# Rewriting the second block of a two-block transformer kernel: three-pass projections, standing gate weights, head-by-head norms

## The reference

```python
h = rmsnorm(x, norm_pre)
proj = h @ w_in          # qa ka va za | qb kb vb ob zb | ig fg | ga gb
oa = diff_attention(qa, ka, va, lam)          # 4 heads; softmax(1) - lam * softmax(2), ALiBi, causal
ya = rmsnorm_heads(oa, norm_a) * (1 - lam_init) * silu(za)
qk = silu(causal_conv4(concat(qb, kb)))
hb = mlstm(qk_q, qk_k, vb, ig + b_i, fg + b_f)   # 4 heads of 128, decay weights, normalised by max(|den|, exp(-m))
yb = rmsnorm_heads(sigmoid(ob) * hb, norm_b) * silu(zb)
merged = sigmoid(ga) * (ya @ w_a) + sigmoid(gb) * (yb @ w_b)
x = x + rmsnorm(merged @ w_out, norm_post)
```

## Time and profile before

| | |
|---|---|
| median of 3 runs | 1297.14 us (1295.32 to 1297.49) |
| the profiled execution | 1300.73 us, its span 1299.5 us |
| PE, PEld busy | 1246.2 us, 1080.4 us |
| DVE, ACT, POOL busy | 946.0 us, 708.5 us, 57.4 us |
| second block, from its first matmul to the span's end | 258.9 us |

### The profile page before, as it was taken

How to read it: one execution, slowest core, us unless ns; L and a number is a source line. 1 busy time by engine, 2 the same in 40 slices (tenths; PEclk the granted TensorE clock), 3 DMA queues, 4 the chain that set the end, 5 groups by cost and what they waited for, 6 DMA issues and landing times.

```text
span 1299.5 us, 18078 instructions
## 1 busy us (share of the span) xinstructions
PE 1246.2 (96%) x7024; PEld 1080.4 (83%) x7024; DVE 946.0 (73%) x1415; ACT 708.5 (55%) x1082; POOL 57.4 (4%) x80
## 2 busy tenths in 40 slices
PE   7999999986999999999999999999999989999977
PEld 6888888875888888888888888988888878878866
DVE  6787666988687776687776667587775677668976
ACT  5665445663565654565554457556554443655463
POOL 4000000010001000000000112000000000000000
PEclk9999999988999999999999999999999998999999
DMA  8766565410366665666655564156655654555430
GB/s 273 230 201 193 165 189 175 162 61 1 114 195 186 187 185 166 199 191 185 192 178 170 174 194 142 50 177 187 189 186 179 188 154 145 163 142 147 134 126 33
DMA packets 201364, 211.42 MB, mean 163 GB/s; under 512 B 8977, under 2 KB 188305, under 8 KB 201279
## 3 DMA queue, kind: packets, MB, share of 16 engines
q1 hardware_dynamic: 198672, 206.66, 52.2%
q10 hardware_dynamic: 2606, 3.60, 0.8%
HBM read 209.19 MB, written 1.05 MB: 162 GB/s over the span
## 4 chain that ended last, share of the span: by engine, by line
PE 79%; DVE 14%; ACT 3%; issue 2%; DMA 1%; POOL 1%; ACTq 0%; SPq 0%; DVEq 0%
PE psum L468 77%; DVE wlo L1812 4%; DVE cv L2028 2%; ACT whi L1221 1%; POOL small L2664 1%; DMA rows<-in_a_ln_b 0%; PE psum L601 0%; ACT pb L1708 0%; PE psum L882 0%; DMA xn<-in_x 0%; DVE small L2377 0%; DVE htmp L1869 0%; ACT qn L1541 0%; DVE pb L2387 0%; PE psum L629 0%
## 5 line engine op out<-in xcount | busy, mean ns | idle before, releaser
L468 PE MATMUL psum<-x,whi 128*128 128x512 f32 x1952 | 696.9, 401 | 16.3 <-DVE htmp L1869 5.0
L1812 DVE TENSOR_TENSOR wlo<-raw,whi 128x1024 fp32r<-128x1024 f32 (+2 forms) x403 | 473.4, 1188 | 161.4 <-ACT whi L1221 157.8
L468 PE MATMUL psum<-x,wlo 128*128 128x256 f32 x1952 | 548.9, 281 | 0.9 <-DVE wlo L1812 0.9
L1221 ACT CAST whi<-raw 128x1024 fp32r<-128x1024 f32 (+2 forms) x403 | 406.5, 1023 | 147.2 <-PE psum L468 137.2
L468 PEld LDWEIGHTS psum<-x,whi 128*128 128x128 f32 x1952 | 370.5, 190 | 107.6 <-DVE htmp L1869 5.7
L468 PEld LDWEIGHTS psum<-x,wlo 128*128 128x128 f32 x1952 | 372.0, 191 | 1.5 <-DVE wlo L1812 1.4
L468 PE MATMUL psum<-g,whi 128*128 128x512 f32 x704 | 247.0, 394 | 0.0
L468 PE MATMUL psum<-g,wlo 128*128 128x256 f32 x704 | 198.2, 282 | 0.0
L468 PEld LDWEIGHTS psum<-g,whi 128*128 128x128 f32 x704 | 132.3, 188 | 30.6
L468 PE MATMUL psum<-whi,x 128*128 128x512 f32 (+2 forms) x544 | 147.5, 370 | 2.0 <-issue 2.0
L468 PEld LDWEIGHTS psum<-g,wlo 128*128 128x128 f32 x704 | 132.4, 188 | 0.0
(11 more groups left out here) (322 smaller groups left out, 950.1 us busy)
## 6 DMA issues: line engine op xcount, KB each, us to landing
raw<-in_ffn_w_gate SPq DMA_DIRECT2D x88, 512.0 KB, 4.5
raw<-in_ffn_w_up SPq DMA_DIRECT2D x88, 512.0 KB, 4.3
raw<-in_ffn_w_down SPq DMA_DIRECT2D x80, 512.0 KB, 4.2
raw<-in_w_in SPq DMA_DIRECT2D x52, 512.0 KB, 4.0
raw<-in_w_o SPq DMA_DIRECT2D x16, 512.0 KB, 3.9
raw<-in_a_w_in SPq DMA_DIRECT2D x14, 512.0 KB, 4.9
raw<-in_w_kv SPq DMA_DIRECT2D x16, 384.0 KB, 3.3
raw<-in_ffn_w_down SPq DMA_DIRECT2D x16, 256.0 KB, 2.7
```

What stands on the lines that cost most here:

```text
L468: return pe.matmul(o, l, r, start=start, stop=stop, skip_group_check=True)
L1221: act.copy(B.whi[:, i % SPLIT, 0:n], B.raw[:, i % RAW, 0:n]).then_inc(*s.hi.now(i))
L1812: dve.tensor_tensor(B.wlo[:, i % SPLIT, 0:n], B.raw[:, i % RAW, 0:n], B.whi[:, i % SPLIT, 0:n].bitcast(F32), ALU.subtract).then_inc(*s.lo. ...
```

## The change

- **Three passes into one place.** The new `direct` sums `hi*xhi`, `hi*xlo` and `lo*xhi` as three 256-column matmuls into the same half bank; `pair` does this for a slot. All column projections of the second block use it (`QK2`, `AQK2`, `GAB2`, `WA2`, `WB2`). There are no halves to add: DVE reads the bank once and scales it. Column pairs get banks of their own (2, 3, 0, 1 for `QK2`; 6, 7, 2, 3 for `AQK2`; 0, 1, 2, 6 and 7, 4, 5, 6 for `WA2`, `WB2`).
- **Gate columns.** The slot `GATE2` is held 128 columns apart (`held`), and its weights stand in PE: 24 matmuls of 256 columns, then two small transposes (`gate_turn`). The decay sums move ahead of `VA2`.
- **Conv.** The first tap goes to ACT (`tap0`, 8 passes); DVE makes three passes per column.
- **Evictions and functions.** One half of `vb` and one of `va` is read by ACT. ACT's order around `VA2` is new: silu of the conv output, one tiny Exp, then the copy of `va`. `rows_steps` does token tile 0 of a slot, then tile 1, and PE signals the first tile's end (`zo0`). All three `z_fn` now stand between the two kinds of jobs.
- **Fewer DVE operations per job.** `tensor_reduce` with negate gives the bias of the exponential directly; the difference is one pass over p with one ratio; the mLSTM's denominator comes out of the product's accumulator.
- **Norms head by head.** ACT squares each head's output with an accumulator (`y_squares`); the gain is multiplied into z once (`z_gain`), and `y_rows` makes one 128x128 pass per head. `GAB_STEPS` sets how many steps of `rest` go with each mLSTM job; the residual's and the first tile's `yb` turns move in among jobs 8 and 9.

```diff
+GAB_STEPS = (2, 2, 2, 1, 1, 2, 2, 1, 1, 1)
...
+    def direct(o, h, l, xi, kc, start, stop, ready=None):
+        mm(o, h, xh[xi][:, kc, :], start, False)
+        mm(o, h, xl[xi][:, kc, :], False, False)
+        if ready is not None:
+            pe.wait_ge(*s.lo.at(ready))
+        return mm(o, l, xh[xi][:, kc, :], False, stop)
...
-    def gate_rows(x):
+    def gate_cols():
...
-        for tt in range(2):
-            o = bank[5 + tt][:, 0:8]
-            for k in range(8):
-                l0, l1 = (x[q][:, k, tt * 128:(tt + 1) * 128] for q in range(2))
-                mm(o, l0, h[:, k, :], k == 0, False)
-                mm(o, l1, h[:, k, :], False, False)
-                t = mm(o, l0, l[:, k, :], False, k == 7)
+        for k in range(8):
+            t = direct(bank[5][:, 0:S], h[:, k, :], l[:, k, :], 0, k, k == 0, k == 7, i if k == 0 else None)
...
     def rest():            # PE
-                pe.wait_ge(*s.sum.at(("gab", c - 2)))
+                pe.wait_ge(*s.gab.at(c - 2))
-                t = block(6 + c % 2, h[:, k, :], l[:, k, :], x[:, k], k == 0, k == 7, i if k == 0 else None)
+                t = direct(bank[6 + c % 2][:, 0:S], h[:, k, :], l[:, k, :], 0, k, k == 0, k == 7, i if k == 0 else None)
...
     def second():          # ACT
+        for i in range(1, 4):
+            use(VA2 + i)
         for h in range(2):
             silu_cols(h)
+        act.activation(small[0:1, 319:320], B.ones[0:1, 0:1], ACT.Exp)
+        act.wait_ge(*s.used.at(VA2 + 3))
+        act.activation(MC.va[:, 0, :], bank[6], ACT.Copy, scale=small[:, 14:15]).then_inc(*s.v_act.now("va"))
...
+        y_squares("a", 7)
+        next(rg)
         z_fn(1, ACT.Sigmoid)
         z_fn(0, ACT.Silu)
-        for _ in range(2):
-            next(rg, None)
+        next(rg)
+        z_fn(2, ACT.Silu)
+        act.activation(small[0:1, 319:320], B.ones[0:1, 0:1], ACT.Exp)
+        next(rg)
...
     def rest():            # DVE
-            dve.tensor_tensor(g, b[:, 0:S], g, ALU.add).then_inc(*s.sum.now(("gab", c)))
-            dve.wait_ge(*s.sum.at(("gab", c)))
-            dve.tensor_tensor(g, g, row_of(6), ALU.mult).then_inc(*s.gab.now(c))
+            dve.tensor_tensor((MC.ga if c < 8 else MC.gb)[:, c % 8, :], bank[6 + c % 2][:, 0:S], row_of(6),
+                              ALU.mult).then_inc(*s.gab.now(c))
...
     def second():          # DVE, mLSTM jobs
+            for _ in range(GAB_STEPS[i]):
+                next(rg)
+            if i == 1:
+                z_gain(0, 0)
+            if i in (2, 3):
+                y_rows("ya", i - 2)
+            if i in (3, 4):
+                turned("ya", i - 3, 4, 1, 0, [3])
+            if i == 4:
+                z_gain(2, 1)
+            if i == 8:
+                y_rows("yb", 0)
```

More of the change, by code:

```diff
@@ L544, in first_use, with rows_steps @@
             pe.wait_ge(*sig.at((gen, c)))
-    def rows_steps(x, gen, K, slot, n, banks, tail=0):
+    def rows_steps(x, gen, K, slot, n, banks, tail=0, first=None):
         kk = SLOT // n
@@ L567, in rows_steps @@
                                    kc == K - 1 and wi == 1)
+                if first is not None and tt == 0 and k0 + kk == K:
+                    t.then_inc(*s.zo0.now(first))
             t.then_inc(*s.used.now(i))
@@ L1102, in second @@
[L1102 to L1105, removed]
+            if c >= 2:
+                pe.wait_ge(*s.qk.at(c - 2))
+            for e in range(2):
+                pair(0, 0, AQK2 + 2 * c + e, (6, 7, 2, 3)[c], range(4 * e, 4 * e + 4), e == 0, e == 1)
+                if c == 0 and e == 0:
+                    gate_turn()
@@ L1629, in mix_b, with tap0 @@
             prep(5, p, [("f3", 6, xh[0])])
+    def tap0(c):
+        act.wait_ge(*s.qk.at(c))
+        for b in (2 * c, 2 * c + 1):
+            t = act.activation(MC.qkc[:, b, :], MC.qk[:, b, 0:S], ACT.Copy, scale=MC.ctap[:, b, 0:1])
+        t.then_inc(*s.tap0.now(c))
     def silu_cols(h):
@@ L1641, in rest @@
                 if k == 3:
-                    z_rows(i)
+                    act.wait_ge(*s.zo0.at(i))
+                    act.activation(MC.zob[:, i, 0, :], bank[6], ACT.Copy, scale=small[:, 14:15]).then_inc(*s.zo_act.now(i))
                 yield
@@ L2454, in ya_steps, with z_gain @@
-    def ya_steps():
-        yield from head128("ya", flat(MC.oa[:]), flat(MC.zob[:, 0]), MC.nab[:, 0, :], 1.0 - LAM_INIT, 200,
-                           flat(MC.aq[:])[:, 0:1024])
-        for tt in range(2):
-            yield
-            turned("ya", tt, 4, 1, 0, [3])
+        dve.reciprocal(small[:, col + 5:col + 6], small[:, col + 4:col + 5]).then_inc(*s.dve_step.tick())
+    def z_gain(i, norm):
+        dve.wait_ge(*s.z_fn.at(i))
+        dve.wait_ge(*(s.ld_nb if norm else s.ld_na).at("all"))
+        z = MC.zob[:, i]
+        dve.tensor_tensor(z, z, wide(MC.nab[:, norm, :], 1, 2), ALU.mult).then_inc(*s.c_dve.now(("zz", i)))
@@ new lines, in y_rows @@
+    def y_rows(g, tt):
+        b = g == "yb"
+        dve.wait_ge(*s.rstd.at((g, tt) if b else g))
+        dve.wait_ge(*s.c_dve.at(("zz", 2 if b else 0)))
+        src = MC.ob if b else MC.oa
+        for h in range(4):
+            q = slice(h * 128, (h + 1) * 128)
+            c = (224 if b else 208) + 4 * tt + h
+            t = dve.scalar_tensor_tensor(out=src[:, tt, q], in0=src[:, tt, q], scalar=small[:, c:c + 1],
+                                         in1=MC.zob[:, 2 if b else 0, tt, q], op0=ALU.mult, op1=ALU.mult)
+        t.then_inc(*s.y.now((g, tt)))
@@ L2476, in second @@
+        for i in range(6):
+            use(QK2 + i)
+        dve.wait_ge(*s.fills.at("qk"))
+        dve.wait_ge(*s.row.at(6))
+        keys(0)
+        keys(1)
+        use(QK2 + 6)
+        keys(2)
+        use(QK2 + 7)
+        use(GATE2)
+        some(cg, 2)
+        keys(3)
+        some(cg, 2)
+        dve.wait_ge(*s.used.at(GATE2))
+        dve.tensor_tensor(MC.oa[0:8, 0, 0:S], bank[5][0:8, 0:S], row_of(6)[0:8], ALU.mult).then_inc(*s.c_dve.now("g8"))
         l12 = MC.lamr[:, 0:3:2, :]
```

605 lines of the change are left out of this document (287 added, 318 removed).

## The result

| | before | after |
|---|---|---|
| median | 1296.23 us (4 runs, 1293.22 to 1297.49) | 1277.36 us (4 runs, 1275.23 to 1281.34) |
| the profiled execution | | 1279.19 us, its span 1277.8 |
| second block, first matmul to the span's end | 258.9 us | 237.09 us |

The ratio is 0.986, with a 95% interval of 0.983 to 0.990: the changed kernel is faster, by 19 us or 1.5%. I had said 1277. The two profiled executions put all of it into the second block: its first matmul starts at 1040.71 us, against 1040.58, and the block is 21.8 us shorter.

What follows compares the result with a forecast made beforehand. PE was taken as the bound, other engines costing time only where PE waits. Terms -9.9 + 1.7 + 0.4 - 1.3 - 9.9 - 1.5 = -20.5 us took the median from 1297.14 to 1276.6, said as 1277; range 1269 to 1288.

Steps and rivals of the forecast that it cites:

- A: Second block's conv, gate, attention and value projections: 84.29 us to become 74.4, a change of -9.9.
- B: Handover to the jobs: 2.38 us to become 4.1 (+1.7), as PE waits for ACT's table loads, silus and copy.
- C: Difference attention with the row projections, 46.57 us: +0.4 net, with 1.45 for a slow restart and 1.0 off for DVE.
- D: mLSTM with merge-gate columns: 63.48 us to 62.2 (-1.3), including new PE waits of 2.1 at the start and 1.1 in job 5.
- E: Products with w_a and w_b: 33.36 us to become 23.5 (-9.9), with yb ready earlier and the banks free.
- F: Output product, 23.37 us: 96 matmuls give 21.8, and late wlo of the last four slots goes, -1.5.
- G: The tail behind the output product, said to stay at 5.47 us.
- Price of one block: Three 256-column matmuls in place of one 512 and one 256: 0.36 us against 0.347, for 320 blocks.
- gate term of 7.1: In A, the new form of the gate rows saves 4.3 us itself and 2.8 in the column pairs behind them.
- slow start: At the start of C, PE restarts slow after its wait on ACT: +1.45 us, bounds 0 and 1.7.
- ACT's bursts are hidden: Rival, chance 0.12: both PE waits on ACT (3.3 and 2.1) and the slow restart fall away, 6.5 less, 1270.5 us.
- a table load holds ACT twice: Rival, chance 0.04: each table load holds ACT twice as long as its row, 5.1 us more, 1282.

Runs made afterwards that it cites:

- half_columns: Changed kernel with each 256-column matmul of the w_a and w_b products split into two of 128, each with its own weight load: 1294.50 us, E 43.32.
- gate_rows: Changed kernel with only the gate columns put back to 48 matmuls of 8 columns, x standing: 1283.58 us, A 78.99 us, 5.13 longer.
- silu_early: Changed kernel with ACT's two silus and the one-element Exp moved right behind the copy of vb: median 1272.81 us, second block 232.67 us.
- fill_wait: Changed kernel with 26 unused 256-column matmuls run while PE waits for ACT's copy of va: median 1277.06 us, second block 235.75 us.
- zfn_late: Changed kernel with ACT's sigmoid and two silus of z moved behind the last cast and the copy of zob: median 1280.89 us, second block 240.61 us.
- gab_2_passes: Changed kernel with DVE reading each merge-gate slot in two passes instead of one: 1278.66 us, D 4.6 us longer.
- run of four passes: Changed kernel with DVE reading each merge-gate slot in four passes instead of one: 1293.03 us, D 16.5 us longer.

## Why the prediction was right

The mechanism held, and the sum came within 1.3 us: the block lost 21.8 us where I had 20.5. That the median lies within 0.4 us of 1277 is in part luck. I had put it 3.6 below the profiled execution, as before the change; it was 1.8 below. These two misses, 1.3 us one way and 1.8 the other, nearly cancel. Stage by stage, against the earlier trace rows:

| | said | came | |
|---|---|---|---|
| A | 84.29 to 74.4 | 73.86 | 0.5 better |
| B | 2.38 to 4.1 | 4.03 | the burst, row for row |
| C | 46.57 to 47.0 | 46.62 | the 1.0 taken off for DVE was not tried |
| D | 63.48 to 62.2 | 61.58 | the wait in job 5 did not come |
| E | 33.36 to 23.5 | 23.55 | |
| F | 23.37 to 21.8 | 21.95 | |
| G | 5.47 | 5.50 | |

- **Price of one block.** 0.360, as taken from the earlier trace rows; and no run gave 0.33, which follows from the gap that the Trainium skill (TensorE: Matmul & The Clock Gate, "Back-to-back issue gap") states for an isolated warm matmul of 256 columns. The 107 ns for a load that the same page of the Trainium skill states ("LDWEIGHTS (loading the stationary operand)") lie near the 0.111 us that a pass took in half_columns. Against the block's 0.347 the form costs 320 x 0.013 = 4 us; the change pays it for banks that need no second half.
- **A.** Nothing waits and the clock stays at 2.4 GHz throughout. The gate term of 7.1 is only in part the narrow form's own (5.1, run gate_rows); what the other 2 came from stays open. As a difference between the two kernels it stood.
- **B and C.** The wait of 3.3 and the slow start are real and separate (runs silu_early and fill_wait). The slow start costs 1.3 to 1.7 us in eight traces and 2.8 in that of zfn_late (C up to its third row group at 35.14 to 35.39 and 36.61, against 33.74 and 33.81 in silu_early and fill_wait). That the slow start would come was inferred from the wait's length; the waits listed further down show that length alone does not decide it. The rival by which ACT's bursts are hidden falls (its 6.5 should have been 3.3 + 2.1 + 1.45 = 6.85), and so does the one by which a table load holds ACT twice: each function starts 0.02 us or less after its load's 1.28. The drain that the Trainium skill (ScalarE: Activation LUTs, "What ACT_TABLE_LOAD costs") adds is in none of these rows.
- **D.** The wait of 2.02 before the first merge-gate slot was foreseen at 2.1. The 1.1 in job 5 was a term too many; the contents are 61.58 - 2.02 = 59.6 and not 59.0. The 128 blocks of before are 128 x 0.347 = 44.4 and not 44.7, so the old waits by that sum were 6.7; yet PE stood idle for only 63.48 - 60.17 = 3.3 of it, and where the rest lay is not shown. That DVE would no longer pace D was right, but the margin was thinner than I had it: without the 16 passes saved in the merge-gate slots D would be 4.6 us longer (run gab_2_passes), so that one edit carries most of what keeps D short. The split between DVE's other savings was not tried.
- **E.** The size was right. Of the two reasons that the prediction named without parting them, the norm's length counts; banks of their own do nothing by themselves. 4.5 of the 9.8 us are put down to no single edit.
- **The sign that was too strict.** The first block's stretch up to 1040.58 was to stay put. It did in the two profiles compared (1040.71), but it moves by 6.3 us among kernels with the same first block, so it could not have told anything.

## What to carry to other kernels

Where another engine frees PE's bank, look at what stands ahead of that read in the engine's written order: a table-loading burst or a split of a later slot there can cost PE time, and moving four such pieces gained 7.5 us more here (block of 229.63 against 237.09). A bank of its own helps only if the reader is late; a shorter reader helps in either case. Price a new form of matmul from any place in the trace that has the same shapes and number of loads, even in another part of the kernel.

## Not expected of the hardware

- 26 extra matmuls in a wait made the second block 1.3 us shorter, since PE did not start again at 1.2 GHz. The length of a wait does not tell by itself: behind waits of 3.26, 2.85, 1.97 and 1.82 us, and 2.68 and 2.08 in the run of four passes, PE went at 1.2 GHz for a while; behind 2.02, 1.65, 1.83 (four passes) and 2.60 it did not.
- Narrow matmuls alone bring it too, with PE never idle: after 4.2 us of 8-column matmuls in one kernel, after 2.9 in the one before.
- At the full clock a matmul of the split products with its own weight load takes 0.111 to 0.112 us from start to start, whether it is 8 or 128 columns wide.
- Stage A repeats to 0.02 us between traces, while the first block's end lies anywhere in 6.3 us, as wide as the spread of the changed kernel's four times (6.1 us). What moves it was not looked into.
